# Mixers whose inputs skip the norm's root: a root row multiplied into each projection job's sums

## What is computed

```python
def rms_norm(x, gain, eps=1e-6):
    y = x * lax.rsqrt(jnp.mean(x * x, axis=-1, keepdims=True) + eps)
    return y * gain

for l in range(2):
    x = x + 0.5 * swiglu(rms_norm(x, ffn1_norm[l]), ...)
    proj = rms_norm(x, mix_norm[l]) @ w_in[l]
    y_rwkv = rwkv7_group(proj[..., :RWKV_IN], ...)      # shift over tokens, lora gates, chunked recurrence
    y_ret = retnet_group(proj[..., RWKV_IN:])           # q, k (rotary), v, gate; retention in chunks of 64
    x = x + concat([y_rwkv, y_ret]) @ w_out[l]
    x = x + 0.5 * swiglu(rms_norm(x, ffn2_norm[l]), ...)
```

## Time and profile before

| | us |
|---|---|
| median of 3 runs | 1422.89 |
| lowest and highest run | 1422.56, 1425.86 |
| the profiled execution | 1426.32 |
| its span, first to last instruction | 1424.4 |
| PE, DVE, ACT busy | 1373.0, 986.8, 780.4 |

### The profile page before, as it was taken

The page is one execution under the profiler, slowest core; times in us unless marked ns, Lnnn a source line. Parts: engine busy times, 40 slices in busy tenths (PEclk is TensorE's granted clock), DMA queues, the critical chain, the costliest instruction groups (busy, mean ns, idle before and its releaser), DMA issues.

```text
span 1424.4 us, 28209 instructions
## 1 busy us (share of the span) xinstructions
PE 1373.0 (96%) x10866; PEld 1185.6 (83%) x10866; DVE 986.8 (69%) x1543; ACT 780.4 (55%) x1296; POOL 9.4 (1%) x23
## 2 busy tenths in 40 slices
PE   7998999999999999999999999999999999999997
PEld 7986887878888889877888887888879987888886
DVE  6977627877666677657766667766677856876665
ACT  6455547766545566435655546555565633655454
POOL 0000000000000000000000000000000000000000
PEclk9999999999999999999999999999999999999999
DMA  8732453245555554203565555556545401465561
GB/s 295 292 123 74 163 212 128 74 150 204 180 193 193 188 177 149 89 4 107 194 205 190 177 194 172 200 192 199 181 152 195 141 19 50 168 215 178 190 200 51
DMA packets 62789, 229.82 MB, mean 161 GB/s; under 512 B 7008, under 2 KB 7264, under 8 KB 62448
## 3 DMA queue, kind: packets, MB, share of 16 engines
q1 hardware_dynamic: 60912, 220.23, 46.0%
q0 software_dynamic: 1792, 8.37, 1.6%
HBM read 227.53 MB, written 1.05 MB: 160 GB/s over the span
## 4 chain that ended last, share of the span: by engine, by line
PE 89%; DVE 6%; ACT 3%; issue 1%; DMA 0%; DVEq 0%; SPq 0%; ACTq 0%
PE PS L793 24%; PE PS L1113 23%; PE PS L1133 16%; PE PS L1115 11%; PE PS L782 1%; PE PS L772 1%; PE PS L1325 1%; PE PS L1319 1%; DVE x_res L1959 1%; DVE out_operands L2055 1%; PE PS L871 1%; DVE w_lo L2033 1%; PE PS L1287 1%; PE PS L859 1%; PE PS L897 1%
## 5 line engine op out<-in xcount | busy, mean ns | idle before, releaser
L1113 PE MATMUL PS<-hT_both,w_hi 128*128 128x512 f32 x1376 | 489.7, 398 | 0.0
L1115 PE MATMUL PS<-hT_both,w_lo 128*128 128x256 f32 x1376 | 386.2, 281 | 0.0
L1113 PEld LDWEIGHTS PS<-hT_both,w_hi 128*128 128x128 f32 x1376 | 258.6, 188 | 62.9
L1115 PEld LDWEIGHTS PS<-hT_both,w_lo 128*128 128x128 f32 x1376 | 259.9, 189 | 3.1
L793 PE MATMUL PS<-hT_both,w_hi 128*128 128x256 f32 x1392 | 255.6, 286 | 2.3 <-DVE w_lo L2033 1.2
L793 PEld LDWEIGHTS PS<-hT_both,w_hi 128*128 128x128 f32 x1392 | 217.8, 192 | 6.6 <-issue 5.2
L2315 DVE TENSOR_TENSOR w_lo<-weight_ring,w_hi 128x1024 fp32r<-128x1024 f32 x176 | 207.1, 1218 | 2.4 <-ACT w_hi L1736 2.4
L793 PE MATMUL PS<-hT_both,w_lo 128*128 128x256 f32 x696 | 197.1, 283 | 0.0
L2321 DVE TENSOR_TENSOR w_lo<-weight_ring,w_hi 128x1024 fp32r<-128x1024 f32 x88 | 107.8, 1225 | 110.4 <-ACT w_hi L1745 110.4
L1736 ACT ACTIVATE w_hi<-weight_ring 128x1024 fp32r<-128x1024 f32 x176 | 175.4, 1045 | 0.0
L2033 DVE TENSOR_TENSOR w_lo<-weight_ring,w_hi 128x1024 fp32r<-128x1024 f32 x107 | 125.8, 1219 | 47.7 <-ACT w_hi L1514 47.4
(11 more groups left out here) (309 smaller groups left out, 1824.0 us busy)
## 6 DMA issues: line engine op xcount, KB each, us to landing
weight_ring<-in_stream SPq DMA_DIRECT2D x411, 512.0 KB, 4.4
norm_gain<-in_gains_in POOLq DMA_DIRECT2D x8, 512.0 KB, 4.1
consts<-in_csts POOLq DMA_DIRECT2D x1, 1864.0 KB, 9.9
arena<-in_taps_in SPq DMA_DIRECT2D x4, 384.0 KB, 3.5
arena<-in_bias_in POOLq DMA_DIRECT2D x1, 1152.0 KB, 12.5
x_res<-in_x_in SPq DMA_DIRECT2D x2, 512.0 KB, 3.8
lora<-in_lora_in POOLq DMA_DIRECT2D x2, 512.0 KB, 3.6
x_out<-yT SPq DMA_DIRECT2D x2, 512.0 KB, 2.7
```

Source lines behind the costliest of these rows:

```text
L1113: pe.matmul(PS[:, b, :], Wh[:, u, k, :], HT2[:, k], start=(k == 0), stop=(k == KT - 1), skip_group_check=True)
L1115: ins = pe.matmul(PS[:, b, 0:T], Wl[:, u, k, :], Hh[:, k, :], start=False, stop=(k == KT - 1), skip_group_check=True)
```

## The change

- `late` counts the mixers too. Their inputs come through `weighted`, and `late_root` and `roots_spread` make the root beside the transposes.
- PE: two matmuls between jobs 0 and 1 make the row of roots in bank 7 (`row_of_roots`). The ACT copies it to `root_row` behind the splits of tiles 2 to 5.
- The copies of jobs 0 to 8, 11 and 12 leave the ACT. On the DVE a new `rooted(n, dst)` multiplies the bank by `root_row`, ahead of each shift, for jobs 7 and 8 ahead of `split_for(9)`, for job 11 ahead of the products `qW` and `kW`, for job 12 behind the masked scores. The silu of jobs 11 and 12 then runs in place in SBUF.
- Jobs 9 and 10 keep their ACT copy, now with the root of each token as its scale, once the DVE has taken out the jobs ahead.
- `root_row` and the diagonals move to the end of the arena, where the mixer has nothing else.
- `added_to_x` asks for a feed-forward phase by name, where it asked `late`.

```diff
-        ROOTS_AT = SPLIT_END + NTT * D + D
+        ROOTS_AT = ARENA - 2 * T - NTT
...
-            return n < len(PHASES) and PHASES[n][0].startswith("ffn")
+            return n < len(PHASES) and (PHASES[n][0].startswith("ffn") or PHASES[n][0] == "mix")
...
+            def row_of_roots(n, b):
+
+                pe.wait_ge(sem("roots_spread"), NTT * (late_before(n) + 1))
+                for t in range(NTT):
+                    ins = pe.matmul(PS[:, b, t * P:(t + 1) * P], cst("ones"), root_diag[:, t, :],
+                                    start=True, stop=True)
+                ins.then_inc(sem("root_row_made"), 1)
...
                 J(0)
+                row_of_roots(n, 7)
                 J(1)
...
+            def root_row_copied(n, b):
+                act.wait_ge(sem("root_row_made"), late_before(n) + 1)
+                act.activation(root_row, PS[:, b, 0:T], ACT.Copy).then_inc(sem("root_row_copied"), 1)
...
-                raw_copy(0)
+                split_to(SPLIT["mix"][2][0])
+                root_row_copied(ph, 7)
                 split_to(SPLIT["mix"][2][1])
...
-                raw_copy(1)
-                raw_copy(2)
+                split_to(SPLIT["mix"][2][2])
...
-                raw_copy(3)
+                split_to(SPLIT["mix"][2][3])
...
                 for n in range(4, 7):
-                    raw_copy(n)
+                    split_to(SPLIT["mix"][2][n])
+                    act.wait_ge(sem("job_made"), jb0 + n - 1)
...
-                act.activation(flat(qR), job_made(jb0, 7), ACT.Copy).then_inc(sem("job_out"), 1)
...
-                act.activation(flat(kR), job_made(jb0, 8), ACT.Copy).then_inc(sem("job_out"), 1)
                 for n in (9, 10):
-                    act.activation(Vret[:, n - 9, :], job_made(jb0, n), ACT.Copy).then_inc(sem("job_out"), 1)
+                    split_to(SPLIT["mix"][2][n])
+                    act.wait_ge(sem("job_out"), jb0 + n)
+                    act.activation(Vret[:, n - 9, :], job_made(jb0, n), ACT.Copy, scale=stat[:, n - 5:n - 4])\
+                       .then_inc(sem("job_out"), 1)
...
                 def gate_made(n):
-                    act.activation(flat(gret[:, 2 * n - 22:2 * n - 20, :]), job_made(jb0, n), ACT.Silu)\
-                       .then_inc(sem("job_out"), 1)
+                    split_to(SPLIT["mix"][2][n])
+                    act.wait_ge(sem("job_out"), jb0 + n + 1)
+                    g = flat(gret[:, 2 * n - 22:2 * n - 20, :])
+                    act.activation(g, g, ACT.Silu)
...
-                if late(n):
+                if PHASES[n][0].startswith("ffn"):
...
+                def rooted(n, dst):
+
+                    dve.wait_ge(sem("job_made"), jb0 + n + 1)
+                    dve.wait_ge(sem("root_row_copied"), late_before(ph) + 1)
+                    dve.tensor_tensor(dst, PS[:, job_bank("mix", n), :].rearrange("p (a t) -> p a t", a=2),
+                                      rep(root_row, 2), ALU.mult).then_inc(sem("job_out"), 1)
...
                     split_for(n)
-                    dve.wait_ge(sem("job_out"), jb0 + n + 1)
                     r = raw[:, n % 2, :, :]
                     if n:
                         dve.wait_ge(sem("shift_made"), 7 * l + n)
+                    rooted(n, r[:, :, 1:T + 1])
+                    dve.wait_ge(sem("job_out"), jb0 + n + 1)
...
                 ins.then_inc(sem("rk_made"), 1)
+                rooted(7, qR)
+                rooted(8, kR)
                 split_for(9)
...
+                dve.wait_ge(sem("job_out"), jb0 + 11)
+                rooted(11, gret[:, 0:2, :])
                 dve.tensor_tensor(flat(qW), flat(qR), cst("QW"), ALU.mult)
                 dve.tensor_tensor(flat(kW), flat(kR), cst("KW"), ALU.mult).then_inc(sem("ret_qk_made"), 1)
...
                     ins.then_inc(sem("st_masked"), 1)
+                rooted(12, gret[:, 2:4, :])
```

More of the change, by code:

```diff
@@ L1118, in gate_up @@
                     if i == 0:
[L1119 to L1123, removed]
+                        row_of_roots(n, 3)
                 def down(i, start, stop):
@@ L1787, in ffn @@
                 act.preload_act_table(ACT.Silu)
-                act.wait_ge(sem("root_row_made"), late_before(n) + 1)
-                act.activation(root_row, PS[:, 3, 0:T], ACT.Copy).then_inc(sem("root_row_copied"), 1)
+                root_row_copied(n, 3)
                 for i in range(SS):
```

## The result

The change made the kernel slower by a little: 1430.02 us (median of 6 runs, 1426.72 to 1434.40) against 1422.79 for the kernel before beside it (1422.56 to 1425.86), a ratio of 1.0033, 95% interval [1.0019, 1.0048]. Forecast were 1423.6 us, between 1420.0 and 1427.0. Two further comparisons of the same two kernels gave 1.0015 [1.0000, 1.0030] and 1.0026 [1.0009, 1.0044], so the excess is 2 to 5 us and not the 7 us that the two first medians suggest. The profiled execution of the changed kernel took 1426.72 us, its span is 1424.9.

A forecast was written before the change was run, and what follows sets the result against it. PE, busy for 96% of the span, was taken as the bound. Per mixer -0.49 + 0.44 + 0.42 = +0.37, for two +0.7 us on the median of 1422.89: 1423.6 us, range 1420.0 to 1427.0 for 8 in 10 runs.

The forecast's parts named there:

- The seam: Ahead of each mixer, inputs no longer wait for the root: 13.85 us becomes 13.36, -0.49 us per mixer.
- the twin: Seam between two feed-forward phases at 863 us, already without the root ahead: 13.36 us, PE's longest gap 0.7 us.
- the whole 2.33 us: PE's wait for the last normed input ahead of the mixer's transposes; its full removal was the far end, -2.33.
- The rival "faster": The whole seam wait goes and the queries' products are done in time: -1.9 us per mixer, 1419.1 us; chance 0.10.
- The root row on PE: Two matmuls behind job 0 cost PE +0.44 us per mixer, between 0.2 and 0.8, without a wait.
- The copies in jobs 0 to 10: Projections: DVE products replace the ACT's copies in jobs 0 to 8, jobs 9 and 10 keep theirs; no cost.
- The rival "slower": The DVE's chain into the turned operands ends late, PE loses 1.0 us more per mixer: 1425.6 us; chance 0.17.
- Job 11: Its DVE product delays the weighted queries and keys, so PE waits ahead of its transposes: +0.42 us per mixer, 0 to 0.7.
- The issue stall: Places where PE stands for issue may move with eight more instructions: bounded at 1.3 us each way and mixer, taken as 0.
- Queues: Paragraph on the gain's load on POOL, SP's loads and PE's eight added instructions; issue stalls taken as 0.
- The clock: Rival: PE's clock falls in the seam's 2.33 us gap, shorter gaps give back up to 1.5 us per mixer, 1420.6; chance 0.02.
- the 0.3% to which I gave 6 in 100: Whole kernel: 0.3%, 4.3 us, is what a measurement can tell from no change; slower by that had chance 0.06.

The follow-up runs named there:

- the run with the products alone: Changed kernel with the old seam, DVE products taken with a row of ones and no root row on PE; ratio 1.0018 to the kernel before, +1.4 us at the same clock.

## Why the prediction was wrong

- **The seam: right.** -0.49 us forecast, -0.49 measured wherever the clock stayed at 1.00, in the three short gaps of the twin; the whole 2.33 us didn't go. The rival "faster" falls.
- **The root row on PE: right.** +0.44 forecast, +0.43 measured (0.42 as one matmul), no wait in front. The row's four records in the timeline of PE, changed kernel:

```profile
513.62 0.60 PE L794 MATMUL PS<-arena,consts 128*128 128x128 f32 x4
```

- **The copies in jobs 0 to 10: right.** PE's stages between the lora matmuls and the turned operands agree to 0.01 us. The rival "slower" named the chain into the turned operands; PE doesn't wait there.
- **Job 11: right in its mechanism, mis-sized in its term.** The path grew by 0.57 + 0.06 = 0.63 us, where I had +0.42. That the trace shows a wait of 0.41 us is luck, for the two aren't the same quantity: the wait counts from the end of the turned operands' train, and before, the transposes began 0.17 us ahead of that end (591.26 + 1.91 against 593.00); 0.41 + 0.17 is the 0.57 to 0.01 us. What I had wrong is the start of the product. I let it begin where the ACT's copy had, 0.20 us behind the first of those records; it began 0.37 us behind them (585.83 and 586.20), and the rest of the DVE's chain took the forecast time. In the run with the products alone it began 0.30 us behind, with 0.34 us of wait and 0.57 of path. Why the DVE starts later than the ACT did, no run tests. +0.2 us a mixer.

```profile
585.83 1.91 PE L1212 MATMUL PS<-consts,arena 128*128 128x128 f32 x16
588.14 0.66 PE L1229 MATMUL PS<-consts,arena 128*128 128x128 f32 x4 [0.41 <-DVE arena L2455]
```

- **The issue stall: the step that failed.** Under "Queues" I wrote that the eight new instructions may move the places where PE stands for issue, bounded it at 1.3 us each way and mixer, and took 0, with no reason given for the 0. In mixer 1 they moved it by four records inside L1411, for nothing; in mixer 2 by eight, which put a stall of 0.53 to 1.08 us on the path (0.75 to 1.29 us on the stretch, in five traces of three kernels). The trace of before would have told it: counting records from the stall in L1406 gives 73 + 48 = 121 to the end of L1432, so with a stall every 127 the next stood 6 records further, behind the wait for the DVE, and eight more records brought it out with two left.
- **The clock: dismissed on one trace.** I gave the clock 0.02, since it was 1.00 in the seam's gap. The kernel before loses it there in one of its two traces. For the forecast this matters twice. The clock falls behind the moved stall in two of the changed kernel's three traces and then costs another 1.6 to 1.7 us; and it spreads the runs of the kernel before over some 10 us, where I took 3.3 us from three runs. The median of 1422.89, on which I built the time, lies 3.6 us under the 1426.5 of the 102 later executions. With it the forecast would have stood at 1427.2, and the excess by the ratios, 0.15 to 0.33%, lies about at the 0.3% to which I gave 6 in 100. Of the 6.4 us by which the first median lies above the forecast, 3.6 are this base, and by the rows below some 1.4 are fixed work (2.1 against my 0.7); the rest is the clock's scatter and its fall behind the stall, which these runs don't separate.

The sum as the runs give it: -0.98 for the seams, +0.86 for the root rows, +1.26 for job 11, +1.0 for the moved stall, 2.1 us at the same clock (2.3 and 2.9 measured), and up to 1.7 more where the clock falls behind the stall.

## What to carry to other kernels

Where an engine's instruction stream stalls at fixed distances, any instruction added, even one that costs nothing where it stands, shifts all the stalls behind it by as many instructions; count from a stall in the trace whether the next one stays behind a wait, and if not, save or add a few instructions. Put the operation that waits for the newest result last among those that could fill its wait, as with job 11 here. And take the scatter of a kernel and the places where its clock falls from several traces before you forecast to a microsecond; stretches of code that the change doesn't touch tell how much of a difference is theirs.

## What the runs showed of the hardware

- PE's stalls for issue stand 256 instructions apart, to within one, in both mixers; a matmul record with its weight load is two. Behind the one ahead of the L1369 at 647.69 us in the kernel before 6 + 2 + 3 + 3 + 1 + 113 = 128 records follow up to the next, at 651.15, with no wait instruction between them. In the 14 traces 32 stalls follow another directly: 11 after 128 records and no wait instruction, 21 after 127 records and one or two. They cost up to 1.8 us where matmuls of 64 columns follow one another. Timeline of PE, kernel before, first mixer:

```profile
647.69 0.39 PE L1369 MATMUL PS<-arena 64*64 64x64 f32 x6 [0.18 <-issue]
647.87 0.27 PE L1406 MATMUL PS<-arena 64*64 64x64 f32 x2
647.91 0.28 PE L1369 MATMUL PS<-arena 64*64 64x64 f32 x3
647.97 0.23 PE L1406 MATMUL PS<-arena 64*64 64x64 f32 x3
648.03 0.22 PE L1369 MATMUL PS<-arena 64*64 64x64 f32 x1
648.03 1.85 PE L1406 MATMUL PS<-arena 64*64 64x64 f32 x113
651.15 0.38 PE L1406 MATMUL PS<-arena 64*64 64x64 f32 x9 [1.26 <-issue]
```

  The Trainium skill has the distance, in "Runtime: NRT & Kernel Launch", section "Instruction fetch mechanics": an engine's instruction memory is refilled in blocks of 256 instructions, and the crossing is "mostly hidden". The traces agree with the distance; hidden it is only behind another wait or where the matmuls are long.
- That the instructions' transfer is what PE waits for can be read too. The page of the changed kernel lists DMA transfers of the kind "instruction" (queue, kind: packets, MB, share of 16 engines), 16 KB each:

```profile
q8 instruction: 64, 1.05, 0.3%
```

  Their times stand in the recorded trace, though in none of its views. Between one stall and the next, in 58 cases, there are exactly as many of these transfers as blocks of 256 instructions, and each of the 86 stalls of 0.15 us and more ends 1.2 to 1.6 us after the last transfer has. In the changed kernel's three traces the transfer was over 2.62, 2.08 and 2.36 us behind the end of the stall in L1411, and the stall in L1437 took 1.08, 0.53 and 0.81 us: the same differences. So where PE is through with 256 instructions before the next 16 KB are there, it stands. No run moved the transfers themselves.
- The granted clock falls to 1.2 GHz behind waits of PE of 0.7 to 2.3 us in some executions and not in others of the same kernel, and 1.2 us of time go with each 0.001 of its mean.
